# Hybrid attention encoder on one core: values of two units projected together with tokens stationary, and another order of the projections among the attention slots

## What is computed

```python
u = rmsnorm(h, g_pre_mix[i])
proj = u @ w_in[i]
qa, ka, va, qb, kb, vb, qc, kc, vc = jnp.split(proj, SPLIT_POINTS, axis=-1)
ya = diff_attention(qa, ka, va, t5_table[:, :A_HEADS], lam, lam_init, subln_g[i])
yb = sliding_window_sink_attention(qb, kb, vb, t5_table[:, A_HEADS:], sinks[i])
yc = chunk_band_attention(qc, kc, vc, c_rel_table[i])
gates = jax.nn.sigmoid(u @ w_gate[i] + b_gate[i])
```

## Time and profile before

| | us |
|---|---|
| median of three executions | 844.64 (844.32 to 844.77) |
| the profiled execution | 844.44 |
| its span, first to last instruction | 842.6 |
| PE busy (matmuls) | 833.5 |
| PE weight loads, beside the matmuls | 728.0 |
| DVE busy | 648.4 |
| ACT busy | 477.6 |
| POOL busy | 400.3 |

### The profile page before, as it was taken

How to read it: one execution, slowest core, us unless ns; L and a number is a source line. 1 busy time by engine, 2 the same in 40 slices (tenths; PEclk the granted TensorE clock), 3 DMA queues, 4 the chain that set the end, 5 groups by cost and what they waited for, 6 DMA issues and landing times.

```text
span 842.6 us, 13358 instructions
## 1 busy us (share of the span) xinstructions
PE 833.5 (99%) x4685; PEld 728.0 (86%) x4685; DVE 648.4 (77%) x1247; ACT 477.6 (57%) x898; POOL 400.3 (48%) x512
## 2 busy tenths in 40 slices
PE   8999999999999999999999999999999999999997
PEld 7888888888888888999998899899999999888885
DVE  6678877788866768966544389988888888799896
ACT  6566666777666664544444447556565655455562
POOL 5454443334444446987677435756565657000002
PEclk9999999999999999999999999999999999999999
DMA  7641223232323213333326631555543443755584
GB/s 216 167 125 55 64 86 99 76 97 82 82 82 82 62 40 88 113 112 109 105 101 210 195 145 51 181 176 173 167 124 118 120 119 120 281 177 185 158 282 160
DMA packets 138790, 109.24 MB, mean 130 GB/s; under 512 B 7559, under 2 KB 122191, under 8 KB 137700
## 3 DMA queue, kind: packets, MB, share of 16 engines
q1 hardware_dynamic: 137242, 101.00, 39.6%
q0 software_dynamic: 576, 4.19, 1.3%
q10 hardware_dynamic: 906, 3.20, 1.0%
HBM read 96.00 MB, written 12.37 MB: 129 GB/s over the span
## 4 chain that ended last, share of the span: by engine, by line
PE 96%; DVE 1%; DMA 1%; POOL 0%; ACT 0%; issue 0%; DVEq 0%; SPq 0%
PE banks L2241 25%; PE banks L2243 24%; PE banks L2242 24%; PE banks L2518 3%; PE banks L2517 3%; PE banks L2516 3%; PE banks L2417 2%; PE banks L2326 2%; PE banks L2325 2%; PE banks L2689 1%; PE banks L2687 1%; PE banks L2688 1%; PE banks L2389 1%; DMA scratch<-in_x_dram 1%; PE banks L2396 1%; PE banks L2380 1%
## 5 line engine op out<-in xcount | busy, mean ns | idle before, releaser
L852 POOL TENSOR_TENSOR ring_lo<-ring_raw,ring_hi 128x256 fp32r<-128x256 f32 x380 | 310.3, 849 | 264.8 <-ACT ring_hi L1008 264.5
L2241 PE MATMUL banks<-u_hi,ring_hi 128*128 128x512 f32 (+1 forms) x624 | 236.4, 379 | 0.6 <-POOL ring_lo L876 0.6
L2243 PE MATMUL banks<-u_hi,ring_lo 128*128 128x512 f32 (+1 forms) x624 | 231.5, 371 | 0.0
L2242 PE MATMUL banks<-u_lo,ring_hi 128*128 128x512 f32 (+1 forms) x624 | 231.3, 371 | 0.0
L2243 PEld LDWEIGHTS banks<-u_hi,ring_lo 128*128 128x128 f32 x624 | 117.5, 188 | 20.7
L2241 PEld LDWEIGHTS banks<-u_hi,ring_hi 128*128 128x128 f32 x624 | 117.7, 189 | 19.3 <-DVE u_lo L1555 0.8
L2242 PEld LDWEIGHTS banks<-u_lo,ring_hi 128*128 128x128 f32 x624 | 117.8, 189 | 18.5
L1008 ACT CAST ring_hi<-ring_raw 128x1024 fp32r<-128x1024 f32 x96 | 100.0, 1044 | 37.4 <-PE banks L2243 23.7
L2069 DVE SCALAR_TENSOR_TENSOR wide<-banks,cols,wide 128x511 f32<-128x511 f32 x88 | 64.7, 744 | 9.7 <-ACT wide L1349 5.9
L859 POOL TENSOR_SCALAR norm_ms<-norm_ss 128x1 f32<-128x1 f32 x15 | 4.8, 319 | 137.7 <-ACT pages L1018 137.6
L2241 PE MATMUL banks<-pages,ring_hi 128*128 128x512 f32 (+1 forms) x176 | 60.1, 341 | 0.0
(11 more groups left out here) (317 smaller groups left out, 1953.1 us busy)
## 6 DMA issues: line engine op xcount, KB each, us to landing
ring_raw<-in_w_ffn_up_dram SPq DMA_DIRECT2D x88, 256.0 KB, 3.5
ring_raw<-in_w_in_dram SPq DMA_DIRECT2D x60, 256.0 KB, 3.3
ring_raw<-in_w_ffn_down_dram SPq DMA_DIRECT2D x55, 256.0 KB, 3.4
ring_raw<-in_w_gate_dram SPq DMA_DIRECT2D x48, 256.0 KB, 3.2
ring_raw<-in_w_out_dram SPq DMA_DIRECT2D x16, 256.0 KB, 3.1
split_tokens<-pages SPq DMA_DIRECT2D x4, 1024.0 KB, 7.1
pages<-split_tokens POOLq DMA_DIRECT2D x4, 1024.0 KB, 11.9
second_tokens<-wide SPq DMA_DIRECT2D x10, 384.0 KB, 4.2
```

The lines of the kernel that those rows point to most:

```text
L852: last = pool.tensor_tensor(wlo[:, r, c], raw[:, r, c], whi[:, r, c].bitcast(F32), ALU.subtract)
L2241: pe.matmul(out, lhs_hi, rhs_hi, start=start, stop=False)
L2242: pe.matmul(out, lhs_hi, rhs_lo, start=False, stop=False)
L2243: return pe.matmul(out, lhs_lo, rhs_hi, start=False, stop=stop)
```

## The change

Values of units 0 to 7 are projected for two units at once. A pair has two tiles, `va` and `vb`, that together hold the weights of 1024 inputs by 256 features: `va` the first four k, `vb` the last four. Here the tokens are the stationary operand (`u_hi[:, k, tok]`, 128 tokens) and the weights move, 256 columns. The result has tokens on the partitions, so ACT casts it straight into the pages of the two units (`v_half`), DVE subtracts for the low part, and `turn_v`, `v_feat` and the copy of the turned bank are left for unit 8 alone. The steps of `va` make tokens 0 to 255 and those of `vb` tokens 256 to 511, and both read both tiles, so both wait for the low part of `vb` and both buffers are free only behind `vb` (`last_user`). The value pages of two pairs alternate (`V_PG`, `V_LATE_PG`).

The order of the tiles is written out in `GEMM_ORDER`, and `STEPS_OF_UNIT` says how many steps each unit takes, in four equal parts. Four tiles (q0, k0, va0, vb0) run ahead of slot 0; unit 0 has 32 steps, units 1 to 7 have 24, unit 8 has 16, units 9 and 10 have 20, unit 11 has 16.

The diff, cut to its core:

```diff
-SLOT_CUTS = {"A": (0, 5, 11, 17, 24), "C": (0, 5, 10, 16, 24), "B": (0, 6, 11, 17, 24)}
+STEPS_OF_UNIT = (32, 24, 24, 24, 24, 24, 24, 24, 16, 20, 20, 16)
+GEMM_ORDER = ("q0 k0 va0 vb0 q1 k1 va2 vb2 q2 k2 q3 k3 va4 vb4 q4 k4 q5 k5 va6 vb6 q6 k6 q7 k7 v8 k8 "
+              "q8 gate0 gate1 q9 gate2 q10 gate3 gate4 q11 gate5 gate6 gate7")
...
 def attention_gemms():
...
+    flat = [(g, k) for g in range(len(tiles)) for k in range(KT)]
+    steps, at = {-1: flat[:RING * KT]}, RING * KT
+    for u, n in enumerate(STEPS_OF_UNIT):
         for qt in range(TT):
-            steps[4 * u + qt] = flat[cuts[qt]:cuts[qt + 1]]
+            steps[4 * u + qt] = flat[at + n * qt // TT:at + n * (qt + 1) // TT]
+        at += n
...
+def last_user(t):
+    return t + 1 if t < len(TILES) and TILES[t][0] == "va" else t
...
 def split_slot(t):
-    return -1 if t < RING else FINISH[t - RING] + 1
+    return -1 if t < RING else FINISH[last_user(t - RING)] + 1
...
                     last.then_inc(proj_act, 1)
+                elif kind in ("va", "vb"):
+                    if n >= 4:
+                        act.wait_ge(pv_done, TT * (n - 2))
+                    for h in range(2):
+                        dst, head = v_half(g, 0, h)
+                        last = act.copy(dst, head)
+                    last.then_inc(proj_act, 1)
                 elif kind == "v":
-                    if n >= 1:
-                        act.wait_ge(v_turned, n)
                     act.copy(v_feat[:], src).then_inc(proj_act, 1)
...
             proj_out(2)
+            proj_out(3)
...
                     w_hi_at(t)
-                if qt == 0 and u <= 8:
-                    act.wait_ge(v_turned, u + 1)
-                    if u >= 2:
-                        act.wait_ge(pv_done, TT * (u - 1))
+                if qt == 0 and u == 8:
+                    act.wait_ge(v_turned, 1)
+                    act.wait_ge(pv_done, TT * (u - 1))
                     act.copy(v_parts(u)[0], turned_v(u)).then_inc(v_hi, 1)
...
                 src = psum[:, proj_bank(g), :]
+                if kind in ("va", "vb"):
+                    dve.wait_ge(proj_act, g + 1)
+                    for h in range(2):
+                        lo, head = v_half(g, 1, h)
+                        last = dve.tensor_tensor(lo, head, v_half(g, 0, h)[0].bitcast(F32), sub)
+                    last.then_inc(v_lo, 1)
+                    return
...
             tables()
-            for g in range(3):
+            for g in range(RING):
                 proj_low(g)
...
                         pe.wait_ge(proj_lo, QK_TILES.index(g - 2) + 1)
+            def v_step(g, step):
+                first = g if TILES[g][0] == "va" else g - 1
+                half = step // 4
+                t = 2 * (g - first) + half
+                out = psum[:, proj_bank(g), 2 * P * half:2 * P * (half + 1)]
+                tok = slice(t * P, (t + 1) * P)
+                for k in (2 * (step % 4), 2 * (step % 4) + 1):
+                    r, c = (first + k // 4) % RING, slice(2 * P * (k % 4), 2 * P * (k % 4 + 1))
+                    mm = triple(out, u_hi[:, k, tok], u_lo[:, k, tok], whi[:, r, c], wlo[:, r, c],
+                                k == 0, k == KT - 1)
...
             def gemm_steps(steps):
...
                     if k == 0:
-                        pe.wait_ge(w_lo_done, g + 1)
+                        pe.wait_ge(w_lo_done, last_user(g) + 1)
                         bank_free(g)
+                    if TILES[g][0] in ("va", "vb"):
+                        v_step(g, k)
+                        continue
...
-                if qt == 0 and u <= 8:
+                if qt == 0 and u == 8:
                     turn_v(u)
```

More of the change, by code:

```diff
@@ L122, in attention_gemms @@
 def attention_gemms():
[L125 to L143, removed]
+    tiles = []
+    for word in GEMM_ORDER.split():
+        kind = word.rstrip("0123456789")
+        tiles.append((kind, int(word[len(kind):])))
+    flat = [(g, k) for g in range(len(tiles)) for k in range(KT)]
+    steps, at = {-1: flat[:RING * KT]}, RING * KT
+    for u, n in enumerate(STEPS_OF_UNIT):
         for qt in range(TT):
-            steps[4 * u + qt] = flat[cuts[qt]:cuts[qt + 1]]
+            steps[4 * u + qt] = flat[at + n * qt // TT:at + n * (qt + 1) // TT]
+        at += n
     finish = {t: s for s, st in steps.items() for t, k in st if k == KT - 1}
@@ L330, in v_page, with v_half @@
         def v_page(u, part):
-            return V_PG + 2 * ((u if u < 8 else 8) % 2) + part
+            if u >= 8:
+                return V_PG + part
+            return (V_PG, V_LATE_PG)[u // 2 % 2] + 2 * (u % 2) + part
+        def v_half(g, part, h):
+            kind, u = TILES[g]
+            bank = psum[:, proj_bank(g), :]
+            ts = slice(0, 2) if kind == "va" else slice(2, 4)
+            page = v_page(u + h, 0)
+            if u < 4:
+                dst = tiled(pages[:, page + part, :])[:, ts, :]
+                return dst, bank.rearrange("p (t h n) -> p t h n", t=2, h=2)[:, :, h, :]
+            flat = pages[:, page:page + 2, :].rearrange("p a n -> p (a n)")
+            dst = flat.rearrange("p (t m a d) -> p t m a d", m=2, a=2, d=CHUNK)[:, ts, :, part, :]
+            return dst, bank.rearrange("p (t h m d) -> p t h m d", t=2, h=2, m=2)[:, :, h, :, :]
         def v_parts(u):
             pair = pages[:, v_page(u, 0):v_page(u, 0) + 2, :]
-            if u < 4:
-                return pair[:, 0, :], pair[:, 1, :]
             flat = pair.rearrange("p a n -> p (a n)").rearrange("p (g a d) -> p g a d", a=2, d=CHUNK)
@@ L696, in _ @@
             for u in range(4, UNITS - 1):
-                bias_before[min(t for t in range(2 * RING, T_ATT) if split_slot(t - RING) >= TT * (u - 1))] = u
+                later = [t for t in range(2 * RING, T_ATT) if split_slot(t - RING) >= TT * (u - 1)]
+                bias_before[min(later, default=T_ATT)] = u
             for t, (kind, n) in enumerate(TILES):
@@ L1174, in _ @@
                     w_hi_at(t)
-                for g in range(3, T_ATT):
+                for g in range(RING, T_ATT):
                     if FINISH[g] == s and (TILES[g][0] == "q" and u >= 8):
```

44 lines of the change are left out of this document (28 added, 16 removed).

## The result

| | us |
|---|---|
| before, median of five executions beside the changed kernel | 844.56 (844.28 to 844.77) |
| after, median of five | 863.96 (862.27 to 864.20) |
| ratio, 95% interval | 1.0224 (1.0212 to 1.0236) |
| the profiled execution of after, its span | 863.96, 862.2 |

The changed kernel is 2.2% slower. The prediction said 0.9%: the sign was right, the time lies 8 us above the range. All of the difference is in the attention. The last turns of weights start at 306.73 us before and at 326.26 after, 19.53 later, and the profiled executions differ by 863.96 - 844.44 = 19.52.

A forecast was written before the change was run, and what follows sets the result against it. PE's own stream was taken as the bound, without idle time. Turns -3.56, narrower matmuls +2.30, slot 0's wait +6.6, clock +2.0, shorter slots +0.5 gave +7.8 on 844.44: 852.3 us, 0.93% slower, range 849.8 to 856.0.

The forecast's parts named there:

- The wait in slot 0: Slot 0: PE stands still from 39.05 to 45.60 for POOL's low part of tile 4, 6.6 us with hand-over.
- The clock behind it: Behind slot 0's wait: PE's clock falls to its lower level, costing 2.0 us, bounds 0 and 2.6.
- The three shortened slots, 7, 15 and 23: Fourth slots of units 1, 3 and 5: softmax weights come late for PE's turns, 0.5 us in all.
- The 384 narrow matmuls: Value tiles: 384 matmuls of 256 columns at 0.120 us replace 192 of 512 columns, 2.30 us more.
- The stream as a whole: PE's own stream: turns removed, -3.56 us, and matmuls exchanged, +2.30 us, together -1.26 us.
- The order of the projections: Slot 0: q1 as tile 4 is split behind slot 0's softmax, so PE waits 6.6 us, once only.
- Slots that become shorter: Fourth slots of units: 0.5 us for units 1, 3 and 5; nothing booked for unit 8, 1 us in range.
- Rival 1: Slot 0's wait comes but the clock holds: 850.3 us, chance 0.18.
- rival 2: Slot 0: ACT splits tile 4 before the softmax, so no wait: 843.7 us, chance 0.04.
- Rival 3: Units 4 to 10: shortened slots run repeatedly into the softmax chain, 4.8 us more, 857 us, chance 0.10.
- PE's idle time is spread over many slots: Sign in the changed trace that the forecast of one idle time of about 6.6 us near 39 us is wrong.
- 2.0 against 1.1 us: Clock loss behind slot 0's wait: 2.0 us kept; 1.1 us if turns don't count as activity for the clock.

The follow-up runs named there:

- even order: Changed kernel with three projections in four slots for units 0 to 8, tiles 4 and 5 cast early, k2, k4, k6 split at once: 844.09 us, 0.9998.
- the second experiment: Changed kernel with ACT's casts of tiles 4 and 5 moved ahead of those of va0 and vb0: 855.71 us, 1.0130.
- The first experiment: Changed kernel with 56 dummy identity turns on PE between slot 0's scores and q1: 862.20 us, 1.0206.
- the last variant: The even order with POOL's two low parts of slot 16 begun only after DVE normalized slot 17's weights: 843.45 us, 0.9985.

## Why the prediction was wrong

**Right.** The wait in slot 0, its cause, place and size (6.28 for 6.6), by copying an old interval behind a new start. The clock behind it (2.5 for 2.0), in part by luck, since nearly the same wait cost 1.7 to 3.0 us by the clock in other runs. The three shortened slots, 7, 15 and 23, and no fourth of their kind (0.70 for 0.5). The 384 narrow matmuls: starts 0.12 us apart (111.88, 112.00, 112.12 above), as taken from the earlier trace rows. By the formula of the Trainium skill (TensorE: Matmul & The Clock Gate, Back-to-back issue gap), which the section gives for an isolated matmul, they would be an estimated 109.2 ns apart; the trace disagrees for this stream. The stream as a whole: about -1.0 for -1.26.

**Wrong: "The order of the projections".** This step followed one tile, tile 4, through the queues of ACT, DVE and POOL, found its wait, and closed with "so the wait occurs once". That holds for POOL's low parts and was taken for all of the order. A projection has more hands behind it than its weights: its bank is read by ACT and DVE in a fixed slot, and the low part of k8 waits for a memset that is tied to slot 28, whatever the order is. Each tile that the table moves moves these too. k8 moved two slots earlier, past the memset on POOL, and brought its wait in front of a softmax on DVE: 4.78 us and 2.1 for the clock, 6.9 us. It could have been read from kernel and trace of before: the finishing slot of k8 in both orders, the line of the memset, and DVE's order in slot 28. The banks of k3, k5 and k7 are the same omission, 2.7 us. Together 9.6 of the 11.7 us by which the sum fell short.

**Wrong in size: "Slots that become shorter".** For slots 24 to 34 nothing was booked, with 1 us in the range for unit 8; 1.25 was measured, 0.93 of it in unit 8. The step looked only at the softmax's weights in front of PE's turns. These three waits are for DVE's low parts (L1678, L1683), in front of the product with the values and of `turn_v`. The even order has none of them; which part of it removed them was not tried apart. The 0.5 for slots 7, 15 and 23 came near for a reason that the step did not see. The passes at which these waits end took 1.17, 1.17 and 1.37 us (after, at 96.61, 144.03 and 192.95) beside POOL's subtractions; with POOL idle the same shapes took 0.75 (even order, 126.35) and 0.88 (before, 217.32). The 1.16 and 1.37 of the earlier trace rows were taken beside POOL too and carry that delay along. It is longer than the waits of 0.23; whether they would go without it was not tried.

**The rivals.** Rival 1, the clock holds, is refuted by the stretches at 0.50, rival 2 by the wait itself; the second experiment made rival 2's condition true, and there the wait was gone. Rival 3 had the right outline, more than one place waits, and a time of 857, but a wrong mechanism: many small waits for the softmax, where beside slot 0 it was a single large one and three for banks. "PE's idle time is spread over many slots" was named as the sign of an error; the sign that came was a second large wait, which the text did not consider.

**Turns and the clock.** The prediction kept 2.0 against 1.1 us because no row separated turns from matmuls. By the Trainium skill (TensorE: Matmul & The Clock Gate, Part 4: PE-mode transpose) turns don't count as PE activity. The first experiment shows them alone: 56 turns through the wait left the clock at 1.00. So turns hold the clock up, and here the measurement decides against the page. Whether turns alone also raise it, on which the 1.1 turned, no run shows.

## What to carry over

When a table of order is changed, list for each moved item every instruction that hangs on it on every engine, with the slots of before and now, and look for those tied to a slot by something else: a memset, a buffer, a bank. An instruction that waits costs what is queued behind it on its engine, so a split that nobody needs yet can hold up a softmax that is due at once. Fewer instructions on the bounding engine bring at most their own time (here 1 us of 844, and only once the waits were removed one by one), while a single wait in a full stream costs several times that, and the clock on top.

## What was not expected of the hardware

The fall of the clock is not a fixed price of a wait. After the scores of slot 0 PE stood still from 39.1 or 39.2 us in three runs with nearly the same wait; the clock fell at 43.48 in after, at 41.00 in the run with k split at once, and at 41.65 in the run with k8 later. The lower level ended in after 5 us behind PE's first matmul, and in the second case 6 us. The loss, half of PE's working time there, was 4.95 / 2 = 2.5, 5.94 / 2 = 3.0 and, in the third, 1.7 us by the row below (its clock in stretches).

```profile
41.65:48.47 6.82, 3.31 (x8) 2.66 (x9) 0.46 (x2) 3.38 (x4) 6.14 (x9) 0.50 0.27 78
```

Why it falls at one time or another these runs don't tell, nor whether this makes the spread of after (862.27 to 864.20, where the last variant has 843.07 to 843.57).

DVE's scaling pass on 256 columns took 0.61 us for a pair with POOL idle and 1.45 beside POOL's subtractions. An off-path engine thus sets the length of a pass on the path, even where no semaphore joins the two. POOL's pieces kept their usual length (5.77 us for eight, 2.86 for four before), so DVE was the one that waited. Only some of its operations were lengthened. In the even order, beside the same pieces, L1737 and L1739, which read a bank, took 0.34 and 0.35 us (at 132.55 and 132.93), as in before; L1742, which reads `scratch` alone, took 0.76 (at 133.31) and 0.29 with POOL idle (at 139.04).
